# Tokens that arrive turned, split beside the first projection, and branches that begin with the convolution's part

## What is computed

```python
z = jnp.einsum('nsd,de->nse', x, w_in)           # q, k, v of three head groups | conv in, B, C | two gates
y_att = combine_groups(outs, lses, xp.dtype)     # dilated band attention, width 512
br_a = jnp.einsum('nse,ed->nsd', y_att, w_branch_attn)
br_c = jnp.einsum('nse,ed->nsd', c_b * z_conv, w_branch_conv)
merged = jax.nn.sigmoid(g_a) * br_a + jax.nn.sigmoid(g_c) * br_c
mix = jnp.einsum('nsd,de->nse', merged, w_out)
h = layer_norm(DEEPNORM_ALPHA * x + mix, ln1_g, ln1_b)
f = peer_ffn(h, ...)                             # product-key retrieval over 16384 single-neuron experts
y = layer_norm(DEEPNORM_ALPHA * h + f, ln2_g, ln2_b)
```

## Time and profile before

| | us |
|---|---|
| median of three executions | 4499.35 (4495.51 to 4501.84) |
| profiled execution | 4500.66 |
| its span, first to last instruction | 4499.1 |
| TensorE busy in the span | 3781.7 (84%) |
| VectorE busy in the span | 3031.3 (67%) |
| `load_x`, first transfer issued to the next stage's first | 1.01 to 30.54 |
| `branches`, first transfer issued to the next stage's first | 1397.45 to 1562.63 |

### The profile page before, as it was taken

The page is one execution under the profiler, slowest core; times in us unless marked ns, Lnnn a source line. Parts: engine busy times, 40 slices in busy tenths (PEclk is TensorE's granted clock), DMA queues, the critical chain, the costliest instruction groups (busy, mean ns, idle before and its releaser), DMA issues. The chain is left out here.

```text
span 4499.1 us, 64773 instructions
## 1 busy us (share of the span) xinstructions
PE 3781.7 (84%) x24917; PEld 3550.5 (79%) x24917; DVE 3031.3 (67%) x5889; ACT 1175.7 (26%) x2134; POOL 1700.7 (38%) x1197
## 2 busy tenths in 40 slices
PE   7999997599998897970674788988888888888887
PEld 7898895499998876870564788888888888888886
DVE  3434433222222344998895899989998999989996
ACT  1313313111111022432892122212222222222221
POOL 0000000000000033775105666667666666666750
PEclk9999998799999998885896899999999999999998
DMA  3122122844443331000248999999999999999994
GB/s 118 37 73 64 26 69 99 307 168 176 163 167 130 127 126 46 28 10 0 113 187 320 350 355 359 356 356 356 354 359 346 367 354 354 361 348 367 353 326 161
DMA packets 434860, 982.93 MB, mean 218 GB/s; under 512 B 48893, under 2 KB 226429, under 8 KB 431522
## 3 DMA queue, kind: packets, MB, share of 16 engines
q0 software_dynamic: 153744, 561.32, 33.4%
q1 hardware_dynamic: 278466, 409.15, 26.2%
q10 hardware_dynamic: 2384, 8.91, 0.5%
HBM read 901.73 MB, written 131.28 MB: 230 GB/s over the span
## 5 line engine op out<-in xcount | busy, mean ns | idle before, releaser
L1920 POOL DMA_INDIRECT u_row<-in_peer_u_dram,eid x512 | 783.6, 1531 | 705.6 <-DVE dots L1979 421.5
L59 PE MATMUL e_ps<-coef_h,v_h 128*128 128x288 f32 x2048 | 660.8, 323 | 245.0 <-DVE v_l L1948 201.2
L59 PE MATMUL e_ps<-hBh,u_h 128*128 128x288 f32 x2048 | 607.3, 297 | 61.7 <-DVE u_l L1941 61.7
L1995 DVE SCALAR_TENSOR_TENSOR f_row<-v_row,g_coef,f_row 128x1024 f32<-128x1024 f32 x508 | 650.6, 1281 | 4.6 <-DMA v_row<-in_peer_v_dram,eid 4.1
L59 PEld LDWEIGHTS e_ps<-coef_h,v_h 128*128 128x128 f32 x2048 | 414.5, 202 | 299.7 <-DVE v_l L1948 247.5
L1926 POOL DMA_INDIRECT v_row<-in_peer_v_dram,eid x512 | 569.6, 1113 | 197.9 <-issue 154.3
L60 PE MATMUL e_ps<-coef_l,v_h 128*128 128x288 f32 x2048 | 634.3, 310 | 0.0
L61 PE MATMUL e_ps<-coef_h,v_l 128*128 128x288 f32 x2048 | 631.9, 309 | 0.0
L1979 DVE CUSTOM_DVE_ANT_0 u_row<-u_row,h_row 128x1024 f32<-128x1024 f32 x512 | 621.0, 1214 | 7.7 <-DMA u_row<-in_peer_u_dram,eid 7.7
L61 PE MATMUL e_ps<-hBh,u_l 128*128 128x288 f32 x2048 | 607.1, 296 | 0.0
L60 PE MATMUL e_ps<-hBl,u_h 128*128 128x288 f32 x2048 | 606.8, 296 | 0.0
(11 more groups left out here) (290 smaller groups left out, 7979.0 us busy)
## 6 DMA issues: line engine op xcount, KB each, us to landing
u_raw<-in_peer_uT_dram SPq DMA_DIRECT2D x128, 512.0 KB, 9.0
v_raw<-in_peer_vQ_dram SPq DMA_DIRECT2D x256, 256.0 KB, 7.7
s_g<-gate_block SPq DMA_DIRECT2D x9, 4096.0 KB, 11.7
x_gate<-s_g SPq DMA_DIRECT2D x64, 576.0 KB
out_o_kv_sample_dram<-in_cache_kv_w_dram SPq DMA_DIRECT2D x32, 1016.0 KB, 7.6
c_raw<-in_conv_tiles_dram SPq DMA_DIRECT2D x40, 512.0 KB, 3.5
w_raw<-in_w_in_dram SPq DMA_DIRECT2D x96, 192.0 KB, 3.7
cache_v<-in_cache_vS_dram SPq DMA_DIRECT2D x8, 2304.0 KB
```

Of the source, the lines that this page charges most:

```text
L59: pe.matmul(out, lh, rh, start=first, stop=False)
L1920: pool.indirect_dma_start(urow[:, r % RING], None, io["peer_u"][0], bass.IndirectOffsetOnAxis(ap=eid[:, r:r + 1], axis=0)).then_inc(urow_i ...
L1995: dve.scalar_tensor_tensor(out=f, in0=vrow[:, r % RING], scalar=coef[:, s % 2, x:x + 1], in1=f, op0=ALU.mult, op1=ALU.add).then_inc(weighe ...
```

## The change

The host hands over two more arrays: `x_tiles`, the prompt's tokens already turned, tile by tile as [128, 8 x 128], and `x_tail`, the same for the 64 sample rows. The stage `load_x` is gone, with its transposes. In `prompt_attn` SyncE loads the nine tiles into buffers that the stage only writes later (`x_raw`), between and behind the two halves of the first weights; the tables and the identity come behind the tiles. ScalarE and VectorE split tile 0 between the two halves of the weights; ScalarE then splits all others at once, VectorE tiles 1 to 3 and then one tile ahead of each `keep`. TensorE waits per tile for `x_lo`. The wait for the tables moves on VectorE from the stage's start to just ahead of the rotations, and TensorE waits for them at its first turn.

In `branches` the first weights are loaded ahead of the attention's output, and split ahead of it on ScalarE and VectorE. In each pass TensorE does the convolution's part of all three chunks first and the attention's part of all three behind it; it waits for `att_lo` between the two, and each chunk's `br_ready` comes with its attention part.

```diff
@@ prompt_attn
+        def x_raw(t):
+            place = ([qT[:, i] for i in range(NG)] + [kT[:, i] for i in range(NG)] +
+                     [vP[:, 4 * i:4 * i + 4].rearrange("p c x -> p (c x)") for i in range(2)] +
+                     [qR[:].rearrange("p a x -> p (a x)")[:, :KD * NS]])
+            return place[t].rearrange("p (k n) -> p k n", k=KD)
...
-            sp.dma_start(cos[:], io["c_cos"].rearrange("p (t c) -> p t c", t=NT)).then_inc(consts, 16)
-            sp.dma_start(sin[:], io["c_sin"].rearrange("p (t a c) -> p t a c", t=NT, a=2)).then_inc(consts, 16)
-            sp.dma_start(mask[:], io["c_mask_prompt"]).then_inc(consts, 16)
...
+            def load_x(t):
+                src = io["x_tiles"][t] if t < PT else io["x_tail"]
+                sp.dma_start(x_raw(t), src.rearrange("p (k n) -> p k n", k=KD)).then_inc(x_in[t], 16)
...
-            load(0, 0)
+            load_half(0, 0, 0)
+            load_x(0)
+            load_half(0, 0, 1)
+            for t in range(1, NT):
+                load_x(t)
+            sp.dma_start(k["ident"][:], io["c_ident"]).then_inc(consts, 16)
+            sp.dma_start(cos[:], ...)
+            sp.dma_start(sin[:], ...)
+            sp.dma_start(mask[:], ...)
@@ prompt_attn, scalar
+            def split_x(t):
+                act.wait_ge(x_in[t], 16)
+                act.activation(k["xTh"][:, :, t * P:t * P + rows_of(t)], x_raw(t), ACT.Copy).then_inc(x_hi, 1)
...
-            split_w(0, 0)
+            split_half(0, 0, 0)
+            split_x(0)
+            split_half(0, 0, 1)
+            for t in range(1, NT):
+                split_x(t)
@@ prompt_attn, vector
-            dve.wait_ge(consts, 48)
+            def split_x(t):
+                cols = slice(t * P, t * P + rows_of(t))
+                dve.wait_ge(x_hi, t + 1)
+                dve.tensor_tensor(k["xTl"][:, :, cols], x_raw(t), k["xTh"][:, :, cols].bitcast(F32),
+                                  ALU.subtract).then_inc(x_lo, 1)
...
-            split_w(0, 0)
+            split_half(0, 0, 0)
+            split_x(0)
+            split_half(0, 0, 1)
+            for t in range(1, 4):
+                split_x(t)
...
                 for t in range(NT):
+                    if s == 0 and t + 4 < NT:
+                        split_x(t + 4)
                     keep(s, t)
...
+                dve.wait_ge(consts, 64)
@@ prompt_attn, tensor
+                if at == 0:
+                    pe.wait_ge(consts, 64)
...
+                        if s == 0 and ri == 0:
+                            pe.wait_ge(x_lo, t + 1)
                         project(s, ri, t)
@@ branches, sync
+            load_w(0)
             for s in range(SP):
                 sp.dma_start(gate[:, s // 2, s % 2], io["s_att"][s]).then_inc(att_in, 16)
-            with sp.Fori(0, KD) as j:
-                sp.wait_ge(w_lo, j + 1)
...
+            with sp.Fori(0, KD - 1) as j:
+                sp.wait_ge(w_lo, j + 2)
+                load_w(j + 1)
@@ branches, scalar (vector alike)
-            act.wait_ge(att_in, 16 * SP)
-            for s in range(SP):
-                act.activation(atth[:, s], gate[:, s // 2, s % 2], ACT.Copy).then_inc(att_hi, 1)
...
             split(0, 0)
+            act.wait_ge(att_in, 16 * SP)
+            for s in range(SP):
+                act.activation(atth[:, s], gate[:, s // 2, s % 2], ACT.Copy).then_inc(att_hi, 1)
@@ branches, tensor
-            pe.wait_ge(att_lo, SP)
...
                     for y, (a, w) in enumerate(CHUNKS):
                         pe.wait_ge(br_done, j * NC + (y + 1 + NC))
+                        for kk in range(KD):
+                            split3(pe, ps[:, NC + y, :w], wh[:, x, SP + kk], wl[:, x, SP + kk],
+                                   k["cvh"][:, kk, a:a + w], k["cvl"][:, kk, a:a + w], kk == 0, kk == KD - 1)
+                    pe.wait_ge(att_lo, SP)
+                    for y, (a, w) in enumerate(CHUNKS):
                         for kk in range(SP):
-                            split3(pe, ps[:, y, :w], wh[:, x, kk], wl[:, x, kk], atth[:, kk, a:a + w],
-                                   attl[:, kk, a:a + w], kk == 0, kk == SP - 1)
-                        for kk in range(KD):
-                            o = split3(pe, ps[:, NC + y, :w], wh[:, x, SP + kk], wl[:, x, SP + kk],
-                                       k["cvh"][:, kk, a:a + w], k["cvl"][:, kk, a:a + w], kk == 0, kk == KD - 1)
+                            o = split3(pe, ps[:, y, :w], wh[:, x, kk], wl[:, x, kk], atth[:, kk, a:a + w],
+                                       attl[:, kk, a:a + w], kk == 0, kk == SP - 1)
                         o.then_inc(br_ready, 1)
```

More of the change, by code:

```diff
@@ L61, in split3 @@
     return pe.matmul(out, ll, rh, start=False, stop=last)
[L65 to L113, removed]
 def prompt_attn(nc, io, k):
@@ L199, in prompt_attn @@
         consts = sem("a_consts")
+        x_in = [sem(f"x_in{t}") for t in range(NT)]
+        x_hi, x_lo = sem("x_hi"), sem("x_lo")
         block = c.enter_context(nc.Block())
@@ L241, in keep_rows @@
                     sp.dma_start(dst, buf[:NS, PT, cols]).then_inc(kv_out, 16)
-            load(0, 0)
+            load_half(0, 0, 0)
[4 more added lines that the diff above has]
+            sp.dma_start(k["ident"][:], io["c_ident"]).then_inc(consts, 16)
+            sp.dma_start(cos[:], io["c_cos"].rearrange("p (t c) -> p t c", t=NT)).then_inc(consts, 16)
+            sp.dma_start(sin[:], io["c_sin"].rearrange("p (t a c) -> p t a c", t=NT, a=2)).then_inc(consts, 16)
+            sp.dma_start(mask[:], io["c_mask_prompt"]).then_inc(consts, 16)
             for s in range(SP):
@@ L288, in _, with split_half @@
         def _(act):
+            def split_half(s, ri, f):
+                act.wait_ge(raw_in[f], (s * 3 + ri + 1) * 64)
+                act.activation(parts(ri)[:, 0, 4 * f:4 * f + 4], raw[:, f], ACT.Copy).then_inc(w_hi_done, 1)
             def split_w(s, ri):
                 for f in range(2):
-                    act.wait_ge(raw_in[f], (s * 3 + ri + 1) * 64)
-                    act.activation(parts(ri)[:, 0, 4 * f:4 * f + 4], raw[:, f], ACT.Copy).then_inc(w_hi_done, 1)
+                    split_half(s, ri, f)
+            def split_x(t):
+                act.wait_ge(x_in[t], 16)
+                act.activation(k["xTh"][:, :, t * P:t * P + rows_of(t)], x_raw(t), ACT.Copy).then_inc(x_hi, 1)
             def split_piece(s, x):
@@ L363, in _, with split_half @@
         def _(dve):
-            dve.wait_ge(consts, 48)
+            def split_half(s, ri, f):
+                dve.wait_ge(w_hi_done, (s * 3 + ri) * 2 + f + 1)
+                hi, lo = (parts(ri)[:, w, 4 * f:4 * f + 4] for w in range(2))
+                dve.tensor_tensor(lo, raw[:, f], hi.bitcast(F32), ALU.subtract).then_inc(w_lo_done, 1)
             def split_w(s, ri):
                 for f in range(2):
-                    dve.wait_ge(w_hi_done, (s * 3 + ri) * 2 + f + 1)
-                    hi, lo = (parts(ri)[:, w, 4 * f:4 * f + 4] for w in range(2))
-                    dve.tensor_tensor(lo, raw[:, f], hi.bitcast(F32), ALU.subtract).then_inc(w_lo_done, 1)
+                    split_half(s, ri, f)
+            def split_x(t):
[3 more added lines that the diff above has]
+                                  ALU.subtract).then_inc(x_lo, 1)
             def split_piece(s, x):
@@ L1079, in _ @@
             dve.sem_inc(br_done, 2 * NC)
[L1080 to L1083, removed]
             def split(j, x):
@@ L1099, in _ @@
             split(0, 0)
+            for s in range(SP):
+                dve.wait_ge(att_hi, s + 1)
+                dve.tensor_tensor(attl[:, s], gate[:, s // 2, s % 2], atth[:, s].bitcast(F32),
+                                  ALU.subtract).then_inc(att_lo, 1)
             with dve.Fori(0, (KD - 2) // 2) as q:
@@ L2218, in program @@
                 k[n] = mixer.enter_context(nc.sbuf_tensor(n, [P, KD, T], F32R))
-            phase(load_x)
             phase(prompt_attn)
@@ L2312 @@
     conv_tiles = _np.ascontiguousarray(conv_tiles).reshape(5, KD, P, D)
+    x_tiles = _np.asarray(inputs["x_prompt"])[0].reshape(PT, P, KD, P).transpose(0, 3, 2, 1)
+    x_tiles = _np.ascontiguousarray(x_tiles).reshape(PT, P, D)
+    x_tail = _np.asarray(inputs["x_sample"]).reshape(NS, KD, P).transpose(2, 1, 0)
+    x_tail = _np.ascontiguousarray(x_tail).reshape(P, KD * NS)
     near, mid, far = (_np.asarray(inputs[f"cache_kv_w{n}"])[0] for n in (128, 512, 2048))
@@ L2318 @@
     for name, a in (*shape_constants().items(), ("peer_uT", u_turned), ("peer_vQ", v_sliced), ("cache_kT", k_turned),
-                    ("cache_vS", v_tiled), ("conv_tiles", conv_tiles)):
+                    ("cache_vS", v_tiled), ("conv_tiles", conv_tiles),
+                    ("x_tiles", x_tiles), ("x_tail", x_tail)):
         arrays[f"in_{name}_dram"] = a
```

16 lines of the change are left out of this document (9 added, 7 removed).

## The result

The changed kernel took 4466.7 us (median of four executions, 4465.47 to 4473.0), the kernel before 4500.6 in the same measurement; the ratio is 0.9933, 95% interval 0.9919 to 0.9947. That is 30 us less, 24 to 36. Two more timings, of five executions each, gave 0.9920 (0.9907 to 0.9934) and 0.9925 (0.9911 to 0.9938). The mean of the three is 0.9926, or 33 us off 4499.35. The forecast was 38.5 us and a time of 4461: the direction and the places were right, the sum about 5 us too large.

The account below looks back on a forecast made before the run. Bound: stretches without TensorE projecting, at the start and ahead of `branches`, behind transfers and splits. 31.0 + 7.5 = 38.5 us off 4500.66 gives 4462; the median lies 1.3 lower, so 4461, range 4454 to 4470.

Parts of the forecast that it names:

- The start: Program start up to the first matmul: it comes at 13.7 us in place of 44.69, a gain of 31.0 us.
- That is 432 KB less: Start: fewer bytes ahead of the first matmul, at 297 GB/s, bring the second weight half's split 1.5 us sooner.
- the stage that is gone: Start: removing `load_x` whole saves 29.53 us; its 18 splits are only moved.
- The moved splits, the tables, the k weights at nothing: Start: splits hide under TensorE's work, and tables and k weights land before they are wanted; cost nothing.
- `branches`, 7.5 us forecast: Start of `branches`: weights issued first land 4.3 us after issue, first matmul at 1405.7 in place of 1413.18.
- Rival (a): `branches`: queue order fails, weights land with the attention's output; gain 1.8 us, time 4467; chance 0.10.
- (b): Start: queue order fails there too, second half lands behind all tiles; first matmul 26.9, time 4480; chance 0.03.
- Rival (c): `branches`: merges at each pass's end starve TensorE seven times; at 6 us each, time 4503; chance 0.02.
- Rival (d): Start: a late tile or slower first fetch holds back the first tiles; a few us, 4465 to 4472; chance 0.07.
- So the slow start stays: `branches`: a start 7.5 us earlier still finds TensorE's clock low, its first 4 us at 1.2 GHz.
- The stages in between only slide: Stages between the start and `branches`: they move earlier, with no term for them in the sum.
- a stage downstream that changes its length: Sign of a wrong prediction: every stage not edited should take as long as before.

Follow-up runs that it names:

- e2: The kernel before with only the changed `branches`, the start left as it was; ratio 0.9983, 7.6 us less.
- e10: The kernel before, unchanged, profiled again; first matmul at 44.0 us, cached attention 125.2 us.
- e11: The kernel before, handed the two new arrays of turned tokens but never reading them; cached attention 124.8 us.
- e13: The kernel before with eleven unused semaphores added; cached attention 127.1 us.
- e15: The kernel before with five unused semaphores added; cached attention 127.8 us.
- e17: The kernel before, unchanged, profiled a third time; first matmul at 43.7 us, cached attention 125.0 us.
- e1: The changed kernel with the whole `branches` of the kernel before, so only the start is edited; ratio 0.9942, 26 us less.
- e3: The changed kernel, unaltered, timed again in five rounds; ratio 0.9920, 36 us less than the kernel before.
- e9: The changed kernel with TensorE's old order in `branches` (attention first), weights still early; 18.1 us from first issue to first matmul, stage 2.4 us longer than before.
- e12: The changed kernel, unaltered, timed once more in five rounds; ratio 0.9925, 34 us less than the kernel before.
- e6: The changed kernel with tile 0 loaded and split behind both halves of the first weights; the text reports that this costs nothing.
- e8: The changed kernel with TensorE starting on the weights' first half, plus unread matmuls while it waits at the start and in `branches`; ratio 0.9915, median 4459.96 us.

## Why the prediction was right, and where it was wrong

**The start, 31.0 us forecast: 28.9 measured.** The mean first matmul of eight profiles with the old start (before, e2, e10, e11, e13, e15 to e17) is 43.7, of five with the new one (changed, e1, e3, e9, e12) 14.8. The chain was right: the same links, released by the same transfer. What failed is the step "That is 432 KB less; at the 297 GB/s of the stretch in which these transfers ran alone, 442 kB take 1.5 us". From the first issue to ScalarE's second split the eight old profiles take 10.7 us in the mean and the five new ones 10.5: the 432 KB brought 0.3 us and not 1.5. The step prices the landing by the bytes in front, and the runs show two things in its place. A stream that begins with weights ran at 137 to 253 GB/s in each of the two microseconds from about 3 to 5 us after its first issue (nine profiles); the old one, which begins with tables, ran there at 293 to 335 in the profile before. And the second half landed when 2.7 MB and not 2.1 had been moved: 0.6 MB of the tiles behind it went ahead of its end, where the old queue had nothing behind. How the 1.2 us divide between the two is not shown: no run kept the queue empty behind the second half.

The other part of the start is the stage that is gone. It was priced at 29.53 us from one profile; over the eight it is 28.0 to 29.5, mean 28.7. The old first matmul at 44.69 was the latest of the eight, 1 us above their mean. 28.7 + 0.3 give the 28.9 but for rounding.

**The moved splits, the tables, the k weights at nothing: right.** ScalarE split the k weights from 26.24 on (forecast: near 32) and TensorE had no wait there. In e6, one profile, even the place of tile 0 doesn't matter.

**`branches`, 7.5 us forecast: 7.5 measured** in the gap ahead of the first matmul (21.1 to 13.6). e9 shows that the early weights alone don't give it. Rival (a) is out: the first weights landed 4.4 us after their issue with the attention's output behind them. So is (b): the second half landed at 11.6 and not behind all tiles, which would have put the first matmul at 26.9. But the order is not strict, as the 0.6 MB of tiles show. Rival (c), starved passes, is out: TensorE has no wait for a merge. Rival (d), given 0.07, named "a slower first fetch", and that is a part of what happened, at 1.1 us in the first matmul (14.8 against 13.7); a tile was never late.

**"So the slow start stays": right that it stays, wrong by 0.6 us in its size.** `branches` from first to last matmul takes 145.0 us in the mean of nine profiles with its new order, in place of 144.4 in eight with the old code. In the two profiles compared, the clock rose 6 us after the start and not 4.3, so that the first 19 matmuls and not 14 ran at 0.32 apart (counted from the spacing: 1413.18 to 1417.50 before, 1379.43 to 1385.35 after). Not all of that is the change's: with the old code the slow spell lasted 4.3 to 5.3 us, with the new 5.0 to 5.9. e8 shows that it comes from TensorE's idleness before and not from the stage's data: matmuls that nobody needs remove it.

**"The stages in between only slide": the second step that isn't borne out.** The cached attention took 1.7 us more in the mean. The prediction itself named "a stage downstream that changes its length" as a sign of being wrong. This is a term missing from the sum, with a size (1.7 us, from ranges that overlap) and without a cause.

The terms as measured: 28.9 + 7.5 − 0.6 − 1.7 = 34.1 us, against 33 by the three timings. The bounds of the sum began at 33.5 us saved, a time of 4466. That 4466.7 still lies in the range of 4454 to 4470 is luck: the range was widened for the spread of the runs and for rival (a), and neither is why the gain was smaller.

## What to carry to other kernels

A start chain priced by the bytes in front needs two more looks: what the stream begins with, and what will stand in the queue behind it. Here 432 KB fewer in front brought 0.3 us in place of 1.5, since the new stream began more slowly and had tiles behind it. A value that comes from one profiled execution has its own spread (1.8 us at the first matmul, 4 us in a stage of mixed transfers and matmuls), and a sum of differences should carry it. When two edits are made so that TensorE can start on one operand before the other is there, price them together: here early weights alone made the stage longer.

## What the runs showed that was not expected

The time for which TensorE stayed at the level of 1.2 GHz after an idle stretch (matmuls 0.32 us apart in place of 0.17) varied from 3.0 us (e17) to 6.2 us (e6) at the start, in the same kernel from 3.0 to 4.6, and from 4.3 to 5.9 us in `branches`; idle matmuls ahead of the real ones took it away at both places. Streams that began with weights ran at 137 to 253 GB/s some 3 to 5 us after their first issue, at a busy share of 0.61 to 1.02, whether they began 1 us or 11.6 us into the program, while the same transfers behind tables ran at 266 to 335 in the profile before. A transfer landed with bytes of later ones moved ahead of it: the weights' second half with 0.6 MB of tiles. And the 5.3 us that the edits of e8 save at two places did not show in the time of the whole: between two executions of one program the cached attention differed by up to 3.8 us, and all behind `branches` by up to 4.7.
